# Even layer: values and gate by halves of the head pairs, some of them among the attention cases; feed-forward and tap order changed too

## The reference

```python
def _swiglu(h, w1, w3, w2):                 # the dense feed-forward, D_FF = 2816
    return (silu(h @ w1) * (h @ w3)) @ w2

# even layer (SSD and dilated attention from one input projection), in words:
#   p = rmsnorm(x) @ even_w_in              columns: z 1024 | xBC 2048 | dt 16 | q k 3072 | v 1536 | gate 512
#   xBC = silu(causal depthwise conv of width 4 over xBC)          ("taps")
#   y   = gated, normed state space output of 16 heads from xBC, dt and z
#   q, k = rotary(rmsnorm per head); three dilation groups (step 1, 4, 16) of 8 heads,
#          one softmax over the keys of all three groups per head place
#   o   = softmax weights @ v, times silu(gate)                    8 heads of 64 columns
#   x   = x + concat(y, o) @ even_w_out
```

## Time and profile before

| | |
|---|---|
| Time, median of 3 runs | 1970.91 us |
| Profiled execution | 1972.29 us |
| Its span | 1970.5 us |
| PE busy | 1903.7 us (97%) |
| DVE busy | 1307.8 us (66%) |
| ACT busy | 941.2 us (48%) |
| POOL busy | 124.5 us (6%) |
| Granted clock of PE, mean | 0.991 |
| Chain that ended last, PE's share | 80% |

### The profile page before, as it was taken

One profiled execution on the slowest core, in us unless ns is written; L12 is line 12 of the kernel. 1 busy time (PEld: TensorE's weight loads), 2 busy tenths in 40 slices (PEclk: granted clock), 3 DMA queues, 4 the chain that ended last, 5 costly groups with the idle time before them and its releaser, 6 DMA issues.

```text
span 1970.5 us, 34244 instructions
## 1 busy us (share of the span) xinstructions
PE 1903.7 (97%) x14547; PEld 1751.3 (89%) x14547; DVE 1307.8 (66%) x1851; ACT 941.2 (48%) x1144; POOL 124.5 (6%) x82
## 2 busy tenths in 40 slices
PE   9999999999999999999999999999989999889999
PEld 9889999999988999988788888888879989779988
DVE  7974566654699547665454558888878556766563
ACT  5353344444444433444444446677756443444464
POOL 0000000000000000000101010101200001100034
PEclk9999999999999999999999999999999999999999
DMA  8221356455532223445444468999954423305420
GB/s 305 86 87 60 108 177 204 160 193 176 175 126 87 73 84 134 167 187 176 164 168 163 169 215 291 322 332 329 334 194 153 143 91 123 124 30 169 137 94 23
DMA packets 52679, 321.84 MB, mean 163 GB/s; under 512 B 6320, under 2 KB 9648, under 8 KB 19760
## 3 DMA queue, kind: packets, MB, share of 16 engines
q1 hardware_dynamic: 52096, 317.76, 46.3%
q10 hardware_dynamic: 432, 1.90, 0.3%
HBM read 317.01 MB, written 1.05 MB: 161 GB/s over the span
## 4 chain that ended last, share of the span: by engine, by line
PE 80%; DVE 13%; ACT 4%; issue 3%; DVEq 0%; ACTq 0%
PE b L383 79%; DVE s_arena L399 5%; DVE s_ring_lo L501 3%; ACT s_wh L408 2%; PE b L2042 1%; ACT s_arena L408 1%; DVE s_arena L1433 1%; DVE s_arena L402 1%; DVE s_arena L2394 0%; DVE s_arena L637 0%; ACT s_arena L405 0%; DVE s_arena L2318 0%; DVE s_roots L399 0%; DVE s_arena L2315 0%; ACT s_arena L411 0%
## 5 line engine op out<-in xcount | busy, mean ns | idle before, releaser
L501 DVE TENSOR_TENSOR s_ring_lo<-s_ring,s_wh 128x2048 fp32r<-128x2048 f32 (+3 forms) x310 | 647.9, 2095 | 323.6 <-ACT s_wh L408 322.7
L408 ACT ACTIVATE s_wh<-s_ring 128x2048 fp32r<-128x2048 f32 (+3 forms) x332 | 574.2, 1732 | 263.4 <-PE b L383 259.8
L383 PE MATMUL b<-s_Hh,s_wh 128*128 128x256 f32 x1832 | 535.1, 292 | 13.9 <-DVE s_ring_lo L501 9.0
L383 PE MATMUL b<-s_Hl,s_wh 128*128 128x256 f32 x1832 | 520.6, 284 | 0.0
L383 PE MATMUL b<-s_Hh,s_ring_lo 128*128 128x256 f32 x1832 | 520.3, 284 | 0.0
L383 PEld LDWEIGHTS b<-s_Hh,s_wh 128*128 128x128 f32 x1832 | 353.3, 193 | 24.4 <-DVE s_ring_lo L501 9.2
L383 PEld LDWEIGHTS b<-s_Hl,s_wh 128*128 128x128 f32 x1832 | 353.9, 193 | 0.5
L383 PEld LDWEIGHTS b<-s_Hh,s_ring_lo 128*128 128x128 f32 x1832 | 353.4, 193 | 0.0
L383 PE MATMUL b<-s_wh,s_arena_r 128*128 128x512 f32 (+1 forms) x964 | 305.3, 388 | 3.2 <-DVE s_arena_r L2234 2.6
L383 PE MATMUL b<-s_arena_r,s_wh 128*128 128x256 f32 x1184 | 216.1, 283 | 8.4 <-DVE s_arena_r L1749 4.6
L383 PEld LDWEIGHTS b<-s_wh,s_arena_r 128*128 128x128 f32 x964 | 180.1, 188 | 41.6 <-DVE s_arena_r L2234 3.9
(11 more groups left out here) (193 smaller groups left out, 1932.7 us busy)
## 6 DMA issues: line engine op xcount, KB each, us to landing
s_ring<-fixed SPq DMA_DIRECT2D x158, 1024.0 KB, 4.9
s_ring<-experts SPq DMA_DIRECT2D x96, 1024.0 KB, 5.1
s_ring<-experts SPq DMA_DIRECT2D x48, 768.0 KB, 4.4
s_ring<-fixed SPq DMA_DIRECT2D x24, 256.0 KB, 4.1
s_c<-c SPq DMA_DIRECT2D x1, 1664.0 KB, 18.0
s_ring<-fixed SPq DMA_DIRECT2D x3, 512.0 KB, 6.2
s_arena<-s_arena SPq DMA_DIRECT2D x48, 32.0 KB, 1.9
s_c<-c ACTq DMA_DIRECT2D x1, 1344.0 KB, 6.2
```

Of the source, the lines that this page charges most:

```text
L383: return e.matmul(out, l, r, start=start, stop=True, skip_group_check=True)
L408: return e.activation(out, x, ACT.Copy, scale=scale)
L501: e.tensor_tensor(l_, r_, h_.bitcast(F), SUB).then_inc(*up(engine, z % "lo", i))
```

## The change

The order of the weight pieces, and of the work that goes with it:

- Dense feed-forward: the down piece of part s-2 stands in slot s (13 slots), not that of part s-1.
- Values and gate: pieces 0, 2, 4 and gate piece 0, then pieces 1, 3, 5 and gate piece 1 (`VALUE_ORDER`). `LATE` is now the step of gate piece 0 (18), so the steps behind it all use B6. The buffers `e_vn` and the counts of placed values go by place in the order, not by number.
- `EVEN`: 32 half steps and 7 turn steps stand ahead of the first "A", 8 half steps among cases 0, 1 and 2, and more turn steps behind case 3.
- Taps: round and rest of a piece stand two steps earlier (at step u those of piece u + 4, from u = 1 to 10).
- Gains ahead of the even layer: on ACT pairs 2 and 3 ahead of the round of xBC piece 1; on DVE the scatter of pair 3 ahead of the gain of pair 2.

```diff
+VALUE_ORDER = (0, 2, 4, 1, 3, 5)
...
-    for j in range(12):
+    for j in range(13):
         if j < 11:
             up("ff", w["ffn_w1"][0], w["ffn_w3"][0], j, 22)
-        if j:
-            down("ff", w["ffn_w2"][0], j - 1, 22)
+        if j >= 2:
+            down("ff", w["ffn_w2"][0], j - 2, 22)
...
-    cols("ev", W, 6160, 7696)
-    cols("eg", W, 7696, 8208)
+    for h in range(2):
+        for j in VALUE_ORDER[3 * h:3 * h + 3]:
+            piece("ev", j, W[:, 6160 + 256 * j:6416 + 256 * j])
+        piece("eg", h, W[:, 7696 + 256 * h:7952 + 256 * h])
...
         def ffn_pe(e):
-            for s in range(12):
+            for s in range(13):
                 if s < 11:
                     up_pe(e, FF, B[0:4], s)
-                if s:
-                    down_pe(e, "ff", lambda k: cut(f_hid, lambda z: z[:, k, :]), s - 1, 22, s == 1)
+                if s >= 2:
+                    down_pe(e, "ff", lambda k: cut(f_hid, lambda z: z[:, k, :]), s - 2, 22, s == 2)
...
-            gain_act(e, 4, 1)
+            for j in (1, 2, 3):
+                gain_act(e, 4, j)
             round_piece(e, li["exbc", 1])
-            for j in (2, 3):
-                gain_act(e, 4, j)
...
-                            if job[1] == 7 and job[2]:
+                            if job[1] == 7 and job[2] in (1, 2):
                                 gain_dve(e, 4, job[2] - 1)
                             scatter_dve(e, *job[1:], job_bank(job))
+            gain_dve(e, 4, 2)
             gain_dve(e, 4, 3)
...
-                    if name == "eo" and t == 2:
-                        for z_ in v_in:
-                            e.wait_ge(z_, 16 * 8 * 3)
+                    if name == "eo" and t in (2, 6):
+                        for z_, n in zip(v_in, (2, 1) if t == 2 else (3, 3)):
+                            e.wait_ge(z_, 16 * 8 * n)
...
-                after.append(("out", li["ev", 3 + u], 2 - u))
+                after.append(("out", li["ev", 2 * u], 2 - u))
...
-        DIL = [("eqk", j) for j in range(12)] + [("ev", j) for j in range(6) for _ in range(2)] + [("eg", j) for j in range(2)]
+        DIL = [("eqk", j) for j in range(12)]
+        for h in range(2):
+            DIL += [("ev", j) for j in VALUE_ORDER[3 * h:3 * h + 3] for _ in range(2)] + [("eg", h)]
+        LATE = DIL.index(("eg", 0))
...
-                    if u % 2 == 0:
+                    n, blk = VALUE_ORDER.index(j), u - first_of[j]
+                    if blk == 0:
                         rounds(e, p)
-                    e.wait_ge(*on("half" if u % 2 == 0 else "used", p))
-                    if j >= 2 and u % 2 == 0:
-                        e.wait_ge(v_in[j % 2], 16 * 8 * (j // 2))
-                    copy(e, e_vn[j % 2][:, u % 2, :], b[:, 0:256]).then_inc(*up("A", "out", p, u % 2))
+                    e.wait_ge(*on("used" if blk else "half", p))
+                    if n >= 2 and blk == 0:
+                        e.wait_ge(v_in[n % 2], 16 * 8 * (n // 2))
+                    copy(e, e_vn[n % 2][:, blk, :], b[:, 0:256]).then_inc(*up("A", "out", p, blk))
...
-        EVEN = "." + ".D" * 25 + "Q" + ".Q" * 12 + "AQR.AQR." + "AQRQ" * 2 + "AQRQQ" * 2 + "ARYARYOYAOYALOOOO"
+        EVEN = "." + ".D" * 25 + "Q" + ".Q" * 6 + "AQR.Q." * 2 + "Q." * 2 + "AQR.Q." + "AQRQQQ" + "AQRQQ" * 2 + "ARYARYOYAOYALOOOO"
...
-                    if u >= 3:
-                        rounds(e, p)
+                    if 1 <= u <= 10:
+                        rounds(e, li[CONV[u + 2]])
...
-                if u >= 3:
-                    rests(e, p)
+                if 1 <= u <= 10:
+                    rests(e, li[CONV[u + 2]])
...
-                j = i - RAW - li["ev", 0] - 1
-                if 0 <= j < 6:
-                    place_values(e, j)
+                for j in range(6):
+                    if i - RAW - 1 == li["ev", j]:
+                        place_values(e, j)
```

More of the change, by code:

```diff
@@ L1773, in ffn_act @@
             rounds(e, li["ff.1", 1])
-            for s in range(12):
+            for s in range(13):
                 def rest():
-                    if s:
-                        rounds(e, li["ff.2", s - 1])
+                    if s >= 2:
+                        rounds(e, li["ff.2", s - 2])
                 if s < 11:
@@ L1793, in ffn_dve @@
             e.tensor_tensor(rt, rt, pcs("nf1").unsqueeze(2).broadcast_to([128, 8, 8]), MUL).then_inc(*up("V", "router gains"))
-            for s in range(12):
+            for s in range(13):
                 def rest():
-                    if s:
-                        rests(e, li["ff.2", s - 1])
+                    if s >= 2:
+                        rests(e, li["ff.2", s - 2])
                 if s < 11:
                     up_dve(e, FF, B[0:4], s, f_e, f_hid, rest)
+                elif s == 11:
+                    rest()
             for j in range(4):
@@ L2553, in y_dve @@
                 yield
-        DIL = [("eqk", j) for j in range(12)] + [("ev", j) for j in range(6) for _ in range(2)] + [("eg", j) for j in range(2)]
+        DIL = [("eqk", j) for j in range(12)]
+        for h in range(2):
+            DIL += [("ev", j) for j in VALUE_ORDER[3 * h:3 * h + 3] for _ in range(2)] + [("eg", h)]
+        LATE = DIL.index(("eg", 0))
+        first_of = {j: min(u for u, z in enumerate(DIL) if z == ("ev", j)) for j in VALUE_ORDER}
         CONV = [("exbc", j) for j in range(8)] + [("edt", 0)] + [("ez", j) for j in range(4)]
-        LATE = 24
         def dil_bank(u):
@@ L2568, in dil_free @@
             if name == "ev":
-                return ("out", li[name, j], v % 2)
+                return ("out", li[name, j], v - first_of[j])
             return ("out", li[name, j])
@@ L2577, in dil_pe @@
                 if name == "ev":
-                    token(e, p, u % 2, b)
+                    token(e, p, u - first_of[j], b)
                     yield
@@ L2626, in dil_dve @@
                 if name == "ev":
-                    if u % 2:
+                    if u - first_of[j]:
                         rests(e, p)
@@ L3137, in place_values @@
         def place_values(e, j):
+            n = VALUE_ORDER.index(j)
             e.wait_ge(*on("out", li["ev", j], 1))
@@ L3142, in place_values @@
                     p0 = 64 * (a % 2) + 32 * h
-                    e.dma_start(e_v[p0:p0 + 32, a // 2, 256 * j:256 * j + 256], e_vn[j % 2][a:128:4, h, :]).then_inc(v_in[j % 2], 16)
+                    e.dma_start(e_v[p0:p0 + 32, a // 2, 256 * j:256 * j + 256], e_vn[n % 2][a:128:4, h, :]).then_inc(v_in[n % 2], 16)
         def sync_program(e):
```

## The result

The changed kernel takes 1976.16 us (median of 20 runs, 1971.76 to 1978.02) against 1971.7 (20 runs, 1970.2 to 1973.28): a ratio of 1.0018, 95% interval 1.0011 to 1.0025. It is slower: by 4.5 us as the medians have it, by 3.6 as the ratio has it. The two differ because the changed kernel's times lie in groups (four near 1972, five from 1974 to 1975.3, eleven from 1976 to 1978). That is about 0.2%, small, but the interval lies above 1.

What follows compares the result with a forecast made beforehand. TensorE bounds the kernel, busy 1903.7 of 1970.5 us. Terms -2.6, -1.3, -5.2 and +8.0 give -1.1; clock falls of +5.4 make +4.3, so median 1975.2 us, own range 1973 to 1979, overall range 1965 to 1980.

Steps and rivals of the forecast that it cites:

- a draw: Rival for the whole kernel: clock falls in one or two gaps only, or case chain 3 us shorter; 1972.3 us, chance 0.35.
- among the cases, up to scores 4: Attention cases from case 0's turn to scores 4: +8.0 us for the halves, plus new clock falls.
- Feed-forward: Dense feed-forward, down pieces one slot later: shorter waits and no wait before the last down piece, -2.6 us without clock falls.
- Gains: Ahead of the even layer: gains before the weight round shorten PE's waits for gained pairs 2 and 3, -1.3 us.
- Tap order: Projection taps: 9.04 us wait becomes 1.7, new 5.0 us gap before the SSD, -5.2 us without clock falls.
- that rival: Taps: the moved round delays piece 1's ACT work and all later rests, adding up to 5 us; at most 1 in 20.
- Values and gate: Late halves among the attention cases: PE idle about 15 us to scores 4 where it was 5.6, costing +8.0 us.
- the bank waits: Cases 0 and 1: second value halves wait for ACT's copy out of the one bank, 3.4 and 1.2 us.
- the placement wait: Before scores 2: value 5 waits for value 1's late-issued placement to free its buffer, 2.5 us idle.
- Clock: New gaps in the feed-forward, before the SSD and among the cases bring falls to low clock, +5.4 us together.
- no one-bank stall, no placement stall: Lower bound among the cases: if ACT and SP never held PE, 7.3 us less, so +0.7 us.
- Interleaving pays: Rival among the cases: late pieces fill the case gaps, whole kernel faster by 11.6 us, 1959.3 us; chance 0.20.

Runs made afterwards that it cites:

- e4: The kernel before with only the feed-forward and gains orders of the change: 1967.02 us, ratio 0.9976 to before.
- e3: The kernel before with only the tap order of the change: 1968.35 us, ratio 0.9982 to before.
- e5: The changed kernel with second halves of the late value pieces in a second bank, B5: 1961.77 us, ratio 0.9956 to before.
- e1: The kernel before with feed-forward, gains and tap orders of the change, values and gate as before: 1962.1 us, ratio 0.9953 to before.
- e7: The changed kernel with both the second bank (e5) and the earlier placement (e6): 1962.79 us, ratio 0.9958 to before.
- e10: e7 with half-step banks turned by one and the first query/key piece started before the last z pieces are done: 1958.49 us, ratio 0.9940 to before.
- e6: The changed kernel with the value placement DMAs issued one piece earlier: 1968.97 us, ratio 0.9989 to before.
- e11: e1 with the same early start of the first query/key piece as e10: 1958.3 us, ratio 0.9930 to before.
- e12: e8 with the same early start of the first query/key piece as e10: 1956.48 us, ratio 0.9921 to before.
- e8: The changed kernel with late halves over three banks, earlier placement, copies before rounds, half steps spread over cases 0 to 5: 1962.84 us, ratio 0.9957 to before.
- e9: The changed kernel, still one bank, with ACT copying late value halves ahead of its weight round: 1970.61 us, ratio 0.9993 to before.

## Why the prediction was right, and where its terms were off

The forecast was slower, 1975.2 within 1973 to 1979, with 0.44 for the side above 1974.8 and 0.35 for a draw; measured 1976.16. The mechanism is right too: the waits that it names are those in the trace, and from case 0's turn to scores 4 it had 61 us where there are 65 (53 before). Counted from the end of the experts, the SSD starts 6.0 us earlier, 6.5 by the sum. Term by term, from the two traces, with the forecast's falls of the clock added to the term that each belongs to (so +10.8 is 8.0 and 2.8):

| | forecast | measured |
|---|---|---|
| feed-forward | -1.6 | -3.6 |
| gains | -1.3 | -1.3 |
| taps, up to the first late turn | -3.6 | -3.5 |
| among the cases, up to scores 4 | +10.8 | +12.05 |
| behind scores 4 | 0 | -1.4 |
| sum | +4.3 | +2.3 (medians +4.5, ratio +3.6) |

- **Feed-forward.** Idle 1.16 and 1.51 for my 1.4 and 2.2; the 0.2 isn't there. The clock did not fall (I had charged 1.0): -3.6 by the even layer's start, where I had -2.6 + 1.0. Right in kind, too small.
- **Gains.** The first wait stayed at 0.75, the second is gone; with the restarts of PE that is the 1.3. Together with the feed-forward it is e4's -4.7.
- **Tap order.** 1.74 for my 1.7, 4.25 for my 5.0; e3 measures -3.5 against -5.2 + 1.6 = -3.6. DVE is the bound from there as worked out. DVE's wait for ACT ahead of the taps of piece 0 is 1.30 us before and after, so no moved round delayed them and that rival is out. Of the clock the forecast saw one side only: behind the new gap PE does 18 matmuls fewer than before in 33 us (2.2 us), but before had a fall of its own from 1580 to 1592 (clock 0.86, about 1.6 us), which the changed kernel doesn't have. Behind the step sizes tanh starts as the table lands; in ACT's timeline of after:

```profile
1512.39 1.28 ACT L408 ACT_TABLE_LOAD   x1
1513.69 0.60 ACT L408 ACTIVATE s_arena<-b 128x512 f32<-128x512 f32 x1
```

  The sum by 1.28 us held, and no drain stands between the load and the tanh. The 2.66 us that the Trainium skill (ScalarE: Activation LUTs, What ACT_TABLE_LOAD costs) gives with a drain would have made the gap longer than 5.0, and it came out shorter.
- **Values and gate.** 2.4 before scores 0 (2.38), the bank waits 3.4 and 1.2 (3.31 and 0.66), the placement wait 2.5 (3.02). The working has 3.6 for the first of these in one place and 3.4 in another; the 3.4 is nearer. Idle to scores 4 was forecast at about 15, 9.4 more than before, and is 13.71, 8.1 more. The term of +8.0 isn't this idle: it has 1.4 us of clock paid back in it.
- **Clock.** My +5.4 over all had 2.8 for new falls in this stretch. Against e5, whose clock stayed at 1.00, PE's time is 4.8 longer, so the falls are mis-sized by 2.0, and the idle by 1.3 the other way. In exchange the feed-forward had no fall. The sum of +4.3 agrees with the +4.5 of the medians to 0.2 us, and that is luck: the feed-forward was 2.0 better and the cases 1.2 worse than forecast, and the ratio itself says 3.6. The agreement of the waits is not luck.
- **Wrong in the working:** I put the placement beside the bank as a second cause, with 2.5 us of its own, and bounded "no one-bank stall, no placement stall" at 7.3 us less, idle only. e5 shows that all three waits reach PE through the one bank, and a second bank is worth 12.2 us with the clock; the late placement makes the third wait as long as it is, but only while there is one bank. The forecast's answer did not hang on this step; what mending the wait would bring did. The price of a wait here is the wait and the fall that may come behind it.
- **Interleaving pays** (0.20): not as the change has it. With a second bank the stretch takes 73.54 us for the 72.26 of before and the 70.73 of e1, and the whole kernel is level with e1, so interleaving shows no gain even then. The Trainium skill (Perfetto Trace Analysis, Optimizing Tensor Performance) wants independent matmul groups to rotate through PSUM banks; e5 is that rule on this kernel: this case's runs agree, with -12.2 us.

## What to carry to other kernels

When matmul steps are moved among work of other engines, look at what must copy out each step's bank and what stands ahead of that copy in its engine's order: here, with one bank, each such chain became a wait of PE, and with two the same late copies and the same late DMA made PE wait no more. Price such a wait at itself plus the stretch of low clock that may follow, and do not add two waits that reach PE through the same resource. Test a change of several parts one part at a time: here three parts worth -9 us were hidden behind one worth +12.

## What was not expected of the hardware

The same gap is not always followed by a fall of the clock. The changed kernel, e7 and e10 have the same program up to here. PE's wait of 1.7 us at 1468 is followed by a fall in the first and the third, and not in e7. Windows of after, e7 and e10:

```profile
1462.00:1475.00 13.00, 11.27 (x82) 11.06 (x81) 12.38 (x20) 9.93 (x12) 0.00 (x0) 0.87 0.43 155
```

```profile
1462.00:1475.00 13.00, 11.27 (x94) 11.07 (x93) 12.17 (x19) 9.93 (x13) 0.00 (x0) 1.00 0.43 157
```

```profile
1462.00:1475.00 13.00, 11.27 (x81) 11.07 (x81) 12.25 (x19) 9.92 (x13) 0.00 (x0) 0.87 0.43 154
```

PE's idle is 1.73 us in each, and the fall costs 12 matmuls in the 13 us, 1.4 us. Ten kernels here have this wait with the same work around it. In their profiled executions five show 0.87 for these 13 us (the changed kernel, e6, e10, e11, e12) and five 1.00 (e1, e5, e7, e8, e9). What decides is not shown by any run here. It may be why the changed kernel's runs spread over 6 us and those of before over 3, but that is only argued.

A fall can also come with no wait of PE near it. Windows of e10 and e12 from 1530 to 1600, where both have the same order of work and PE is busy throughout:

```profile
1530.00:1600.00 70.00, 70.00 (x512) 63.37 (x511) 38.91 (x62) 32.60 (x45) 0.00 (x0) 0.98 0.31 106
```

```profile
1530.00:1600.00 70.00, 70.00 (x525) 63.37 (x525) 39.97 (x63) 33.59 (x47) 0.00 (x0) 1.00 0.31 106
```

In e10 the clock is 0.79 from 1570 to 1578, and 13 matmuls fewer are done in the 70 us. The kernel before has such a fall from 1580 to 1592. So not every fall can be charged to a wait, and a term for the clock stays a chance.

A fall ahead of a wait cost nothing. Windows from scores 0 to the second half of value piece 1, of after and of e6:

```profile
1664.01:1672.88 8.87, 5.34 (x40) 4.52 (x40) 6.28 (x17) 4.39 (x8) 1.45 (x2) 1.00 0.40 137
```

```profile
1662.83:1671.71 8.88, 6.61 (x41) 5.87 (x41) 6.12 (x17) 4.40 (x8) 1.46 (x2) 0.81 0.15 64
```

In e6 PE did this at clock 0.81 and was busy 1.27 us longer, and its wait was 2.27 us for 3.31: the stretch is as long in both, since ACT's chain sets its end.

SP's eight small placement DMAs took 5.74 us to issue in the changed kernel against 4.92 in rows 10, and 7.08 us from their start to the copy that waits for them against 6.33: their time isn't constant.
